# Gated linear attention in steps among the projections of the second block, tiles of two delta heads put away in DRAM, and the delta heads' norm in halves

## The chip, the cores and the metric

The kernel runs on one core of a Trainium2 chip. The metric is the device time of one execution in microseconds (us). The engines are PE (TensorE), DVE (VectorE), ACT (ScalarE), POOL (GpSimd) and SP (SyncE), which here issues all DMAs.

## What is computed

Two transformer blocks follow each other on x of 1024 tokens by 1024 features, all float32. The change touches only the mixer of the second block:

```python
proj = h @ w_in
(dn_q, dn_k, dn_v, dn_z, dn_a, dn_b, gl_q, gl_k, gl_v, gl_g, gl_r) = split(proj)
qkv = silu(causal_dwconv(concat(dn_q, dn_k, dn_v), dn_conv))
o_dn = gated_delta_rule(l2_norm(q), l2_norm(k), v, log_a, beta)          # 4 heads of 128
o_dn = rms_norm(o_dn, dn_norm_g) * silu(dn_z)
log_alpha = log_sigmoid(gl_r @ gla_w_gate2 + gla_b_gate) / 16
o_gla = gla_attention(gl_q, gl_k, gl_v, log_alpha)                       # 4 heads, keys of 64, values of 128
o_gla = rms_norm(o_gla, gla_norm_g) * silu(gl_g)
y = concat(o_dn, o_gla) @ w_o
```

In chunks of 64 tokens, gla_attention is: b = cumsum(log_alpha); att = causal((q exp(b)) (k exp(-b))^T); the state S over the chunks, S = S exp(b_last) + (k exp(b_last - b))^T v; and o = att v + (q exp(b)) S.

## The kernel before, in words

All activations lie transposed: features on the 128 partitions, 1024 tokens along the free axis. A dense product (product_steps, line 427) makes one tile of 128 output features. Weight tile and activation are each split in a high and a low part, and for each of 8 k tiles six matmuls of 512 columns run (high by high, low by high, high by low, two halves each), 48 a product. The list PLAN fixes the order of all weight tiles. At the start of product i (begin_sp, begin_act, begin_dve) SP issues the load of tile i + 5 once the low half of tile i + 2 is made, ACT casts the high part of tile i + 2 and DVE subtracts its low part. Each engine runs its own program in the written order, and semaphores tie them together. Everything in a program stands behind what is written ahead of it.

PSUM is used in four pairs of banks. Pairs 0 to 2 (the list dense) go round; a taker waits for the last reader of the pair.

The second block's mixer has these stages, one behind the other:

1. **Projections** (proj_pe, proj_act, proj_dve, proj_sp): 29 products: a small one (28: delta gates and GLA rank), then for each delta head h the tiles q (h), k (4 + h), v (8 + h), z (12 + h), then for each GLA pair hp (two heads share a tile of keys) gq (16 + hp), gk (18 + hp), two gv (20, 21 + 2 hp), two gz (24, 25 + 2 hp). Behind a q, k or v product stand a copy out of PSUM, a convolution on DVE (lines 2616, 2619), silu and, for q and k, a square on ACT (2520, 2525), a sum over partitions on PE (439), the root on ACT (453, 455) and a scaling on DVE (2625). These later parts run behind the next product (the list later). V is turned into token order (445) and scaled by beta to VT. z and gz go through silu to DRAM (spill), as gq and gk of the second pair do.
2. **Prep** (prep_*): the delta rule's triangular inverses, two rounds of four groups.
3. **Delta chunks** (delta_*): the KT tiles, then eight chunks of 128 tokens, four heads each. PE makes p1 (line 2848), DVE rd (2902), PE p2 (2855), ACT vn (2880), PE p3 and the output (2863, 2865), DVE the state S (2915), ACT the copy od (2883).
4. **GLA and norms** (gla_*, norm_*): drive interleaves three generators, one for each GLA pair and one for the four delta norms, a step of each in turn. A GLA pair has gates on PE (3022) and four passes on ACT; a scan and differences on DVE (3099 to 3109); three exponentials (3072 to 3075); kd, q and k scaled on DVE (3118 to 3121); kd turned (445); scores (3035) and their mask (3128); 15 states (3043) with two DVE updates each (3137), one PSUM pair per state; and the outputs of two heads (3052, 3055), eight groups of one matmul with att and two with the state. Then come square, sum, root, gate for each head, and the split in high and low parts for w_o.
5. **w_o** (o_*): eight products over the eight heads, in the order of O_ORDER, with the residual lanes X1 fetched from DRAM. Then the layer norm and the second FFN.

```python
            delta_pe(pe)
            drive([gla_pe(pe, 0), gla_pe(pe, 1), norms(pe, norm_pe)])
            o_pe(pe)
...
        O_ORDER = (4, 5, 6, 7, 0, 3, 1, 2)
            for c in range(15):
                r = slice(64 * (c % 2), 64 * (c % 2) + 64)
                ps = psum.take(pe, dense, f"gls{hp}{c}", ("gl_S", hp, c, 1))
```

## Time and profile before

| | us |
|---|---|
| median of 3 runs (lowest, highest) | 3825.42 (3822.31, 3826.05) |
| the profiled execution | 3833.62 |
| its span, first to last instruction | 3831.9 |
| PE busy in the span | 3604.6 (94%) |
| DVE, ACT busy | 1658.3 (43%), 1161.2 (30%) |

The profile is one execution. A matmul with float32 operands appears in it as two records, so "x16" of such a line are eight instructions; a matmul of the dense products (high and low parts) is one record. "PEclk" is the clock that TensorE was granted, as a share of its full 2.4 GHz. A value in brackets behind a row of the timeline is the idle time of that engine before it, and what it waited for.

### The profile page before, as it was taken

The page shows a single profiled execution, that of the slowest core. Times are in us where ns is not written, and L with a number is a line of the kernel's source. Part 1 is how long each engine was busy: PE and PEld are TensorE (multiplying, and loading weights), DVE is VectorE, ACT ScalarE, POOL GpSimd, SP SyncE. Part 2 cuts the span into 40 slices and gives each one's busy share as a digit, 9 for nine tenths or more (in the row PEclk, how much of TensorE's full clock was granted, in tenths as well). Part 3 has the DMA queues.
Part 4 walks back from the last instruction along what each step waited for, and adds up shares of the span by engine and source line. Part 5 has one row for each costly group of instructions (what it writes and reads, how often), then busy time and mean ns, then how long its engine had stood idle before and what let it go on. Part 6 is the DMA issues. An engine that isn't in the chain of part 4 may idle for free.

```text
span 3831.9 us, 38735 instructions
## 1 busy us (share of the span) xinstructions
PE 3604.6 (94%) x16598; PEld 2913.9 (76%) x16598; DVE 1658.3 (43%) x2021; ACT 1161.2 (30%) x1588; POOL 25.2 (1%) x69
## 2 busy tenths in 40 slices
PE   7999999989999999999999979998979899999997
PEld 5778887777766688888888757888957588888785
DVE  6544443224554333323233454317653453434354
ACT  3232213332356522111111274314332331212122
POOL 0000000000000000000000000000000000000000
PEclk9999999999999999999999999999967999999998
DMA  2214241113300121111111121120012011111111
GB/s 104 57 50 144 86 148 37 48 42 116 114 22 28 47 80 66 44 55 40 54 44 51 48 75 55 61 72 6 1 39 83 28 47 53 43 51 44 50 40 54
DMA packets 78011, 223.20 MB, mean 58 GB/s; under 512 B 12024, under 2 KB 22008, under 8 KB 77824
## 3 DMA queue, kind: packets, MB, share of 16 engines
q1 hardware_dynamic: 77840, 220.72, 17.3%
q8 instruction: 131, 2.15, 0.2%
q14 instruction: 40, 0.33, 0.0%
HBM read 196.32 MB, written 23.19 MB: 57 GB/s over the span
## 4 chain that ended last, share of the span: by engine, by line
PE 83%; DVE 8%; ACT 7%; DMA 1%; issue 1%; SPq 0%; ACTq 0%; DVEq 0%
PE PS L427 69%; PE PS L439 2%; PE PS L2725 1%; PE PS L2713 1%; PE PS L3055 1%; PE PS L1743 1%; PE PS L445 1%; PE PS L3052 1%; ACT dS L1511 1%; PE PS L1462 1%; PE PS L1765 1%; PE PS L854 1%; DVE xlo L461 1%; DVE GS L3137 1%; PE PS L2718 0%
## 5 line engine op out<-in xcount | busy, mean ns | idle before, releaser
L427 PE MATMUL PS<-xhi,whi 128*128 128x512 f32 x3120 | 997.9, 401 | 54.6 <-DVE xlo L461 43.2
L427 PE MATMUL PS<-xlo,whi 128*128 128x512 f32 x3120 | 970.1, 392 | 0.0
L427 PE MATMUL PS<-xhi,wlo 128*128 128x512 f32 x3120 | 967.9, 392 | 0.0
L427 PEld LDWEIGHTS PS<-xhi,whi 128*128 128x128 f32 x3120 | 584.9, 190 | 198.3 <-issue 55.3
L427 PEld LDWEIGHTS PS<-xlo,whi 128*128 128x128 f32 x3120 | 592.1, 190 | 126.1
L427 PEld LDWEIGHTS PS<-xhi,wlo 128*128 128x128 f32 x3120 | 590.2, 189 | 125.3
L392 DVE TENSOR_TENSOR wlo<-raw,whi 128x1024 fp32r<-128x1024 f32 (+3 forms) x307 | 329.9, 1076 | 471.2 <-ACT whi L387 471.2
L387 ACT CAST whi<-raw 128x1024 fp32r<-128x1024 f32 (+3 forms) x307 | 284.9, 929 | 514.6 <-PE PS L427 490.5
L427 PE MATMUL PS<-fhi,whi 128*128 128x512 f32 x704 | 219.3, 393 | 8.5 <-DVE flo L461 8.5
L427 PE MATMUL PS<-flo,whi 128*128 128x512 f32 x704 | 218.1, 391 | 0.0
L427 PE MATMUL PS<-fhi,wlo 128*128 128x512 f32 x704 | 218.0, 391 | 0.0
L427 PEld LDWEIGHTS PS<-fhi,whi 128*128 128x128 f32 x704 | 133.1, 190 | 37.7 <-DVE flo L461 10.2
L427 PEld LDWEIGHTS PS<-flo,whi 128*128 128x128 f32 x704 | 133.2, 189 | 28.0
L427 PEld LDWEIGHTS PS<-fhi,wlo 128*128 128x128 f32 x704 | 133.0, 189 | 27.8
L458 ACT CAST fhi<-fuv 128x1024 fp32r<-128x1024 f32 x44 | 46.2, 1050 | 328.4 <-DVE fuv L2135 221.8
L427 PE MATMUL PS<-yhi,whi 128*128 128x512 f32 x352 | 111.0, 397 | 7.6 <-DVE ylo L461 7.6
L427 PE MATMUL PS<-ylo,whi 128*128 128x512 f32 x352 | 109.8, 393 | 0.0
L427 PE MATMUL PS<-yhi,wlo 128*128 128x512 f32 x352 | 109.7, 393 | 0.0
L2202 DVE TENSOR_SCALAR fcb<-fsg,V 128x1024 f32<-128x1024 f32 x44 | 35.8, 814 | 163.6 <-ACT fsg L2178 163.6
L2218 DVE SCALAR_TENSOR_TENSOR merged<-PS,mod,merged 128x1024 f32<-128x1024 f32 x32 | 41.1, 1284 | 151.3 <-PE PS L427 151.3
L2142 DVE TENSOR_TENSOR merged<-PS,merged 128x1024 f32<-128x1024 f32 x32 | 39.2, 1225 | 137.7 <-PE PS L427 137.7
L2178 ACT COPY fsg<-PS 128x1024 f32<-128x1024 f32 x44 | 44.8, 1018 | 173.7 <-PE PS L427 173.6
(474 smaller groups left out, 3762.8 us busy)
## 6 DMA issues: line engine op xcount, KB each, us to landing
raw<-in_w_up SPq DMA_DIRECT2D x88, 512.0 KB, 3.2
raw<-in_w_in SPq DMA_DIRECT2D x67, 512.0 KB, 3.3
adr<-in_w_ada SPq DMA_DIRECT2D x48, 512.0 KB, 4.7
raw<-in_w_gate SPq DMA_DIRECT2D x32, 512.0 KB, 3.3
raw<-in_w_down SPq DMA_DIRECT2D x32, 384.0 KB, 3.1
raw<-in_w_down SPq DMA_DIRECT2D x32, 320.0 KB, 2.9
raw<-in_w_br SPq DMA_DIRECT2D x24, 256.0 KB, 2.7
spill<-wk SPq DMA_DIRECT2D x10, 512.0 KB, 4.2
```

The costliest lines, as they stand in the source:

```text
L387: act.e.copy(whis[i % RING][:, 0:kt, :], raws[i % RING][:, 0:kt, :]).then_inc(*give("w_hi", i))
L392: dve.e.tensor_tensor(wlos[i % RING][:, 0:kt, :], raws[i % RING][:, 0:kt, :], whis[i % RING][:, 0:kt, :].bitcast(F32), ALU.subtract).then_ ...
L427: ins = pe.e.matmul(ps[:, h * 512:(h + 1) * 512], w[s][:, k, :], x[:, h * 512:(h + 1) * 512], start=(at == 0 and n == 0), stop=(at == kt - ...
L439: ins = pe.e.matmul(ps[:, h * 512:(h + 1) * 512], ones, x[:, h * 512:(h + 1) * 512], start=first, stop=last)
L445: ins = pe.e.transpose(ps[:, j * 128:(j + 1) * 128], src[:, j * 128:(j + 1) * 128], ident)
L458: act.e.copy(dst, src).then_inc(*give(*signal))
L461: dve.e.tensor_tensor(dst, src, hi.bitcast(F32), ALU.subtract).then_inc(*give(*signal))
L854: ins = pe.e.matmul(o, H[m][rows, n, :], CL[m][rows, i, 1:9, :].rearrange("p a b -> p (a b)"), start=False, stop=(m == 1), skip_group_chec ...
L1462: ins = pe.e.matmul(ps[:, 64 * h:64 * h + 64], dP[u % 2][:, n, k, :], Vt[:, k0 // 128 + k, 64 * h:64 * h + 64], start=(k == 0), stop=(k == ...
L2142: dve.e.tensor_tensor(X2[:, ft, :], psum.of(j), X2[:, ft, :], ALU.add).then_inc(*give("f1_x", c, ft))
L2178: act.e.copy(GSG[v][:, FPAD:], psum.of(j)).then_inc(*give("f2_raw", v, i))
L2218: dve.e.scalar_tensor_tensor(X1[:, ft, :], psum.of(j), gt_f(ft), X1[:, ft, :], ALU.mult, ALU.add).then_inc(*give("f2_x", c, ft))
```

## The change

The order of the projections becomes a table, PROJ, in which the first GLA pair stands ahead of delta heads 0 and 1, and the second pair between heads 1 and 2 (gz tiles come behind the first z of a pair of heads). Its place in the table is called the slot. A GLA pair is cut in 13 steps, one a slot, at the head of the slot's code on each engine; the first pair starts in slot 2, the second in slot 16. The states of one step share PSUM pairs, four to a pair. Since the GLA tiles need room, q, k and VT of heads 0 and 1 are put away in DRAM in slots 8 to 15 and fetched from slot 26 on; the finished GLA heads go to DRAM too and come back as the low half XH[1] of w_o's operand, where they are split during the first four delta chunks. The norm of the delta heads is made in halves of 512 tokens: the first half of head f during chunk 4 + f, the second behind the chunks. w_o starts with the first four k tiles (the GLA heads) of three products.

The slots are: 0 small; 1 gq, 2 gk, 3 and 4 gv; 5 q0, 6 k0, 7 v0, 8 z0; 9, 10 gz; 11 q1, 12 k1, 13 v1, 14 z1; 15 to 28 the same for the second pair and heads 2 and 3.

```diff
+PROJ = [("small", 28)]
+for _hp in range(2):
+    PROJ += [("gq", 16 + _hp), ("gk", 18 + _hp), ("gv", 20 + 2 * _hp), ("gv", 21 + 2 * _hp)]
+    for _h in (2 * _hp, 2 * _hp + 1):
+        PROJ += [("q", _h), ("k", 4 + _h), ("v", 8 + _h), ("z", 12 + _h)]
+        if _h % 2 == 0:
+            PROJ += [("gz", 24 + 2 * _hp), ("gz", 25 + 2 * _hp)]
...
+        G_STEPS = ("gate", "sum", "exp", "kd", "kT", "at", "st0", "st1", "o0", "o1", "sq", "root", "d")
+        G_FROM = (2, 16)
+
+        def gla_steps(eng, gla, slot):
+            for hp in range(2):
+                if 0 <= slot - G_FROM[hp] < len(G_STEPS):
+                    gla(eng, hp, G_STEPS[slot - G_FROM[hp]])
...
+            def states(c0, n, ring):
+                ps = psum.take(pe, ring, f"gls{hp}{c0}", ("gl_S", hp, c0 + n - 1, 1))
+                pe.wait_ge("gl_kdt", hp)
+                pe.wait_ge("vt", 21 + 2 * hp)
+                for c in range(c0, c0 + n):
+                    r = slice(64 * (c % 2), 64 * (c % 2) + 64)
+                    x = 512 * (c % 2) + 256 * ((c - c0) // 2)
+                    ins = pe.e.matmul(ps[:, x:x + 256], kdt[hp][r, c // 2, :], vt[r, c // 2, :], start=True, stop=True)
+                ins.then_inc(*give("gl_s", hp, c0))
...
+        PARKED = [FT[0][0], FT[0][1], FT[1][0], FT[1][1], VT[0], VT[1]]
+        PARK_AT = {8: (0,), 9: (1,), 10: (4,), 14: (2,), 15: (3, 5)}
...
+            for slot, (kind, ft) in enumerate(PROJ):
+                gla_steps(pe, gla_pe, slot)
+                project(ft, ("sm",) if kind == "small" else (UNTIL[kind], ft))
...
+        def norm_pe(pe, ring, f, hf):
+            ps = bank.take(pe, ring, f"gn{f}{hf}", ("gn_root_ln", f, hf))
+            pe.wait_ge("gn_sq", f, hf)
+            pe.e.matmul(ps, ones, nrm[f][hf], start=True, stop=True).then_inc(*give("gn_ss", f, hf))
...
         def delta_pe(pe):
...
+                if c >= 4:
+                    norm_pe(pe, ring, c - 4, 0)
+            for f in range(4):
+                norm_pe(pe, ring, f, 1)
...
         def delta_act(act):
...
-            for s in range(10):
+            for s in range(4):
                 act.wait_ge(f"away{s}", 0)
+            begin_act(act, "w_o", 0)
             for c in range(8):
+                if c > 4:
+                    root(act, c - 5, 0)
...
+                if c < 4:
+                    other_hi(act, 4 + c)
+                else:
+                    squares(act, c - 4, 0)
+            squares(act, 0, 1)
+            squares(act, 1, 1)
+            root(act, 3, 0)
+            squares(act, 2, 1)
+            squares(act, 3, 1)
...
         def delta_dve(dve):
...
+                if c < 4:
+                    other_lo(dve, 4 + c)
+                else:
+                    gated(dve, c - 4, 0)
+                    if c > 4:
+                        normed(dve, c - 5, 0)
...
-        O_ORDER = (4, 5, 6, 7, 0, 3, 1, 2)
+        O_ORDER = (4, 5, 6, 7, 0, 1, 2, 3)
...
         def o_pe(pe):
+            first = [product_steps(pe, dense, "w_o", ft, OX, ("x1", ft), order=O_ORDER) for ft in range(3)]
+            for steps in first:
+                for _ in range(4):
+                    next(steps)
...
-            drive([gla_pe(pe, 0), gla_pe(pe, 1), norms(pe, norm_pe)])
```

The instruction order shows three places. In the changed kernel line numbers differ: 431 is 427 before, 443 is 439, 449 is 445, 391 is 387, 457 and 459 are 453 and 455.

PE, at the end of the delta chunks. Before, behind the last four output matmuls (AT by small) the GLA gates begin (g is the second gate matrix, sm the small projection):

```order
L2865 MATMUL PS<-AT_285,small_315 128x128
L2865 MATMUL PS<-AT_285,small_317 128x128
L2865 MATMUL PS<-AT_285,small_319 128x128
L2865 MATMUL PS<-AT_285,small_321 128x128
L3022 MATMUL PS<-sm_228,g_224_272 128x512 x4
```

Now, behind them, the norm sums (nrm, ones) and at once the first k tile of w_o (xhi, xlo are its operand, whi, wlo the weights):

```order
L3150 MATMUL PS<-AT_313,small_349 128x128
L3070 MATMUL PS<-nrm_364,ones_54 128x512
L3070 MATMUL PS<-nrm_359,ones_54 128x512
L3070 MATMUL PS<-nrm_361,ones_54 128x512
L3070 MATMUL PS<-nrm_363,ones_54 128x512
L3070 MATMUL PS<-nrm_365,ones_54 128x512
L431 MATMUL PS<-xhi_65,whi_60 128x512 x2
L431 MATMUL PS<-xlo_66,whi_60 128x512 x2
```

Between the delta chunks and w_o no GLA instruction is left on PE; five norm matmuls of 512 columns stand there.

PE, between two products of the projections, slots 8 to 9 (wk is the work tile of a convolution or of V, gv and kdt are values and turned keys of GLA):

```order
L431 MATMUL PS<-xhi_65,wlo_63 128x512 x2
L449 MATMUL PS<-ident_50,wk_274 128x128 x8
L2432 MATMUL PS<-gv_284,kdt_292 128x256 x7
L431 MATMUL PS<-xhi_65,whi_61 128x512 x2
```

The seven state matmuls of step st1 stand between V's transposes of slot 8 and the product of slot 9; before, only the transposes stood between products.

ACT, slot 16 (gA, gB are GLA's work tiles, gk its keys, gq its queries, whi the cast of a weight tile):

```order
L2790 ACTIVATE gq_281<-PS 128x1024
L391 CAST whi_61<-raw_58 128x1024
L2481 ACT_TABLE_LOAD
L2485 ACTIVATE gA_289<-PS,V_49 128x1024
L2487 ACTIVATE gB_291<-gA_289 128x1024
L2489 ACTIVATE gB_291<-gB_291 128x1024
L2491 ACTIVATE gB_291<-gB_291 128x1024
L2790 ACTIVATE gk_283<-PS 128x1024
```

The step's four passes stand behind the cast for product i + 2 and ahead of the copy of the slot's own product (gk).

## Rows read from the trace of the kernel before

**Rows 1.** The page, part 4: the chain that ended last, by engine.
```profile
PE 83%; DVE 8%; ACT 7%; DMA 1%; issue 1%; SPq 0%; ACTq 0%; DVEq 0%
```
**Rows 2.** Windows by stage: busy us (instructions) of each engine, granted clock, DMA.
```profile
core 0: us, PE busy (x) PEld busy (x) DVE busy (x) ACT busy (x) POOL busy (x), PEclk, DMA share, GB/s
2249.80:2585.00 335.20, 331.67 (x1458) 267.77 (x1458) 110.35 (x105) 129.28 (x129) 0.00 (x0) 0.99 0.22 75
2741.00:2784.50 43.50, 39.29 (x327) 36.99 (x326) 22.60 (x65) 16.64 (x63) 0.00 (x0) 1.00 0.01 1
2784.50:2930.20 145.70, 117.80 (x372) 82.84 (x371) 64.40 (x100) 49.07 (x52) 0.00 (x0) 0.61 0.18 69
2810.00:2823.00 13.00, 13.00 (x65) 12.78 (x64) 9.01 (x10) 4.78 (x6) 0.00 (x0) 0.50 0.00 0
...
2855.00:2913.50 58.50, 57.61 (x194) 46.01 (x194) 3.17 (x4) 3.06 (x4) 0.00 (x0) 0.50 0.05 18
...
161.20:169.40 8.20, 8.20 (x49) 6.38 (x47) 0.00 (x0) 0.00 (x0) 0.00 (x0) 1.00 0.18 71
```
**Rows 3.** Timeline at the borders of stages: start, length in us, engine, line.
```profile
2584.65 3.23 DVE L2763 TENSOR_SCALAR wb<-ones,g 128x128 f32<-128x128 f32 x16 [8.52 <-PE PS L427]
...
2585.67 3.81 PE L2685 MATMUL PS<-upper,wb 128*128 128x128 f32 x32 [1.06 <-DVE wb L2763]
...
2783.42 1.06 PE L2865 MATMUL PS<-AT,small 128*128 128x128 f32 x8
...
2930.28 1.19 PE L427 MATMUL PS<-xhi,whi 128*128 128x512 f32 x2 [5.98 <-DVE xlo L461]
```
**Rows 4.** The chain in order of time: one product of the projections; all of w_o.
```profile
2561.89 10.93 PE PS L427 x48
...
2930.28 89.97 PE PS L427 x384
```
**Rows 5.** Timeline, PE: prices of the kinds of matmul that move, and a like group.
```profile
2291.45 1.88 PE L439 MATMUL PS<-wk,ones 128*128 128x512 f32 x4
...
2262.20 1.04 PE L445 MATMUL PS<-ident,sm 128*128 128x128 f32 x8
...
2819.94 3.62 PE L3035 MATMUL PS<-gq,gk 64*128 64x128 f32 x16
...
2872.73 0.79 PE L3052 MATMUL PS<-gat,gv 128*128 128x128 f32 x2
2873.46 1.11 PE L3055 MATMUL PS<-gq,GS 64*128 64x64 f32 x4
2874.50 0.79 PE L3052 MATMUL PS<-gat,gv 128*128 128x128 f32 x2
...
162.14 0.49 PE L852 MATMUL PS<-Mk,Ug 128*128 128x128 f32 x2
162.56 0.71 PE L854 MATMUL PS<-CL,H 64*128 64x128 f32 x4
163.19 0.49 PE L852 MATMUL PS<-Mk,Ug 128*128 128x128 f32 x2
```
**Rows 6.** Timeline of the projections: the chain behind a q product of head 1.
```profile
2328.00 1.28 ACT L2528 ACT_TABLE_LOAD   x1
...
2333.46 3.92 DVE L2619 SCALAR_TENSOR_TENSOR FT<-wk,V,FT 128x1023 f32<-128x1023 f32 x3
...
2338.58 1.06 ACT L2525 ACTIVATE wk<-FT 128x1024 f32<-128x1024 f32 x1
...
2339.78 1.95 PE L439 MATMUL PS<-wk,ones 128*128 128x512 f32 x4 [0.21 <-ACT wk L2525]
...
2340.60 1.23 DVE L392 TENSOR_TENSOR wlo<-raw,whi 128x1024 fp32r<-128x1024 f32 x1 [3.22 <-ACT whi L387]
```
**Rows 7.** Timeline of the delta chunks: a chunk's last od, the next p1 and rd.
```profile
2764.37 0.27 ACT L2883 COPY wk<-PS 128x128 f32<-128x128 f32 x1 [0.18 <-PE PS L2865]
...
2764.89 1.13 PE L2848 MATMUL PS<-small,FT 128*128 128x128 f32 x8 [0.56 <-ACT wk L2883]
2765.39 1.13 DVE L2902 SCALAR_TENSOR_TENSOR small<-PS,g,VT 128x128 f32<-128x128 f32 x4 [0.89 <-PE PS L2848]
```
**Rows 8.** One line's instructions: copies of 512 columns on ACT, ns min/median/max.
```profile
L2746 ACT COPY wb<-PS x48: 586/587/588, 2608.4 to 2736.7; 128x512 f32<-128x512 f32 x48
```
**Rows 9.** Groups by line, DVE: the state updates: busy us, mean ns.
```profile
L3137 DVE SCALAR_TENSOR_TENSOR GS<-GS,gbl,PS 64x128 f32<-64x128 f32 x60 | 20.8, 347 | 22.9 <-PE PS L3043 20.1
```

More of the change, by code:

```diff
@@ L2389, in proj_sp @@
+        def proj_sp(sp):
             puts = iter(range(8))
-            def project(ft):
+            for slot, (kind, ft) in enumerate(PROJ):
                 begin_sp(sp, "w_in2", ft)
-                for _ in range(4):
-                    k = next(puts, None)
-                    if k is not None:
-                        sp.wait_ge("put", k)
-                        sp.e.dma_start(spill[:, k, :], X2[:, k, :]).then_inc(*land(f"lane{k}", "spill"))
-            def away(ft):
-                project(ft)
-                sp.wait_ge("z_out", ft)
-                sp.e.dma_start(spill[:, 8 + SLOT[ft], :], work_tile("z", ft)).then_inc(*land(f"away{SLOT[ft]}", 0))
@@ new lines, in proj_sp @@
+                if slot == 15:
+                    store_heads(sp, 0)
+                for n in PARK_AT.get(slot, ()):
+                    x = PARKED[n].rearrange("p a b -> p (a b)") if n >= 4 else PARKED[n]
+                    sp.wait_ge(*PARK_OF[n])
+                    sp.e.dma_start(spill[:, 16 + n, :], x).then_inc(*land(f"lane{n}", "park"))
+                if slot == 26:
+                    sp.wait_ge("gl_oc", 1, 1)
+                    for n in range(4):
+                        sp.wait_ge(f"lane{n}", "park")
+                        unparked(sp, n)
@@ L2629, in token @@
                 if ft < 16:
[L2630 to L2632 removed]
                     h = ft - 8
+                    if h < 2:
+                        dve.wait_ge(f"lane{h}", "spill")
+                    else:
+                        dve.wait_ge("gn_d", 4, 0)
+                        dve.wait_ge("gl_S", 0, 14, 1)
                     dve.wait_ge("beta")
@@ L2820, in build @@
         rb_ = small[16:20]
+        half = [slice(0, 512), slice(512, 1024)]
+        zD = [mem("zD", at_ft(2 * h), [128, 2, T]) for h in range(4)]
+        nrm = [[mem("nrm", heap + h * TB, [128, 512]), mem("nrm", at_ft(2 * h) + TB // 2, [128, 512])] for h in range(4)]
         def chunk(c):
@@ L2827, in group, with delta_sp @@
             return 4 * (h // 2) + c // 2, sl[2 * (c % 2) + h % 2]
+        def delta_sp(sp):
+            for r in ROUNDS[1]:
+                sp.wait_ge("pp_tx", r, 6)
+            for n in range(4):
+                sp.wait_ge(f"away{4 + n}", 0)
+                sp.e.dma_start(XH[1][:, 4 + n, :].bitcast(F32), spill[:, 12 + n, :]).then_inc(*land(f"away{4 + n}", "back"))
+            for h in range(4):
+                sp.wait_ge("rc_o", 3, h)
+                sp.e.dma_start(zD[h][:, :, 0:512], spill[:, 8 + h, :].rearrange("p (a b) -> p a b", a=2)).then_inc(*land(f"away{h}", "back"))
@@ new lines, in root, with head_hi, gated @@
+        def root(act, f, hf):
+            act.wait_ge("gn_ss", f, hf)
+            inverse_root(act, nrm[f][hf], bank.of(f"gn{f}{hf}"), 128, ("gn_root", f, hf), tables=False)
+        def head_hi(act, f, hf):
+            act.wait_ge("gn_d", f, hf)
+            if hf == 0:
+                act.wait_ge("rc_v", 7, 3)
+                act.wait_ge("rc_o", 7, 3)
+            hi_of(act, XH[0][:, f, half[hf]], od_half(f, hf), "ox_hi", f, hf)
+        def gated(dve, f, hf):
+            dve.wait_ge("od", 4 * hf + 3, f)
+            dve.wait_ge(f"away{f}", "back")
+            z = zD[f][:, hf, 0:512]
+            dve.e.scalar_tensor_tensor(z, od_half(f, hf), vec("dn_g"), z, ALU.mult, ALU.mult).then_inc(*give("gn_z", f, hf))
```

723 lines of the change are left out of this document (363 added, 360 removed).

## The prediction

> **What bounds the kernel now.** I read the chain that ended last first: PE holds 83% of the span, DVE 8%, ACT 7% [rows 1]. Time is therefore won only where PE waits or runs at its lower clock. The windows by stage show where that is [rows 2]. In the projections (2249.8 to 2585.0) PE is busy 331.7 of 335.2 us at clock 0.99: nothing to win there. The delta chunks (2741.0 to 2784.5) also run at clock 1.00. The stage behind them, 2784.5 to 2930.2, is 145.7 us with PE "busy" 117.8 us but at a mean clock of 0.61. It holds both GLA pairs and all eight norms, and it ends in a wait: the first product of w_o starts at 2930.28, the last delta matmul was running until 2784.48 [rows 3]. Inside it, 2855.0 to 2913.5 is 58.5 us of the GLA outputs alone at clock 0.50. Two things cost time here: the work itself, at half clock, and latency between PE, ACT and DVE. 117.8 us at 0.61 is about 72 us of work at full clock, so about 74 us of the stage is lost.
>
> **What the change takes away.** The stage goes. Between the last delta matmul and w_o now stand 145.8 us (2930.28 - 2784.48) [rows 3]. What stays is a tail. After the last od copy (0.3 us behind that matmul) ACT makes four half squares and one half root before PE can run the last of its norm matmuls: six half passes at 0.59 us [rows 8], 3.5 us, and some semaphore time, 4.2 us in all. The last norm matmul takes 0.94 us (two took 1.88 [rows 5]). So w_o starts about 5.7 us behind the last delta matmul. The rest of the tail (the other half roots, eight casts, the DVE halves) runs some 13 us on ACT, under the first four k tiles of three w_o products: 72 matmuls, or 1.5 products of 10.93 us [rows 4], 16.4 us. So it stays hidden. Gain 145.8 - 5.7 = **140.1 us**. w_o itself took 89.97 us for 384 matmuls, which at 10.93 us a product would be 87.4 [rows 4]: its beginning ran at half clock. After the short tail most of that goes: **2.0 us** more, at least 0 and at most 2.6.
>
> **What it adds in the projections.** PE is full there, so every matmul that moves in costs its full price, at full clock:
> - gates: four matmuls of 512 columns, 0.94 each [rows 5]: 3.8
> - transposes of kd: two sets of eight, 1.04 each [rows 5]: 2.1
> - scores: 32 matmuls of 64 rows by 128 columns. Eight (16 records) took 3.62 us at half clock [rows 5], 0.45 each, so 0.226 each: 7.2
> - states: 30 of 256 columns, half the price of 512, 0.47: 14.1
> - outputs: 32 groups of one 128-row matmul and two of 64 columns. A group took 1.77 us at half clock (2872.73 to 2874.50), so 0.885 if it scales. The nearest shape at clock 1.00 is the first block's group of L852 and two L854, 1.05 us (162.14 to 163.19), with wider matmuls [rows 5]. I take 0.95, nearer to the row of the same shape: 30.4, between 28.3 and 33.7
> - sums of squares: eight of 512 columns, 0.94: 7.5
>
> That is **65.1 us**. It agrees with the 72 us of work above, less eight such matmuls (7.5) for the delta norms.
>
> Do the waits hide? The other engines' part of the moved work is large: on DVE some 29 us a pair (30 state updates at 0.35 [rows 9], five gate passes, nine more full passes), on ACT some 21 us. They are spread over 13 slots (a slot is one product with what stands around it), and both engines were busy only 110 and 129 us of 335 [rows 2]. The tight place is the convolution chain. From the end of a product ACT copies, loads a table (2328.00), takes the root, DVE scales and convolves (2333.46, 3.92 us), ACT does silu and the square (2338.58), and PE, done with the next product, waited 0.21 us for it [rows 6]. That chain is 12.8 us and a slot of q or k is 10.93 + 1.88 = 12.8 us: no slack now. After the change the slots that carry a GLA step on PE are longer by it (1.8 to 7.6 us), which gives the chain slack just where ACT and DVE get more to do. I walked slots 5 to 14 with these durations: ACT and DVE hold GLA steps for slot n before they reach the copy of slot n, so they fit in the idle time before a product's end. I find one wait of some 0.4 us a pair, at the transposes behind slot 14 (28 for the second pair), whose own slot has no PE step: **+1 us**. One early wait of about 3 us goes, because small, gq and gk now stand in the slots where ACT also writes the residual lanes: **-3 us**, bound 0.
>
> The queues: SP now issues 12 transfers more of 512 KB (six tiles put away, six fetched), a second scan mask, and four fewer (gq and gk of the second pair, away and back). The load for product i + 5 waits, as before, for the low half of i + 2, one slot's work; of the tiles put away only V of head 1 is awaited on ACT soon after (slot 16, gate). I expect that wait to end inside slot 16, with nobody on PE needing it before slot 20. 0 us.
>
> **The border to the prep stage.** Before, the last products were gate tiles with little behind them: DVE started the first log-decay tiles at 2584.65 and PE followed at 2585.67, 1.05 us behind [rows 3]. Now the last slots are q3, k7, v11, z15. In slot 28 the silu of v11 ends about 11.3 us in; then come the cast (1.03), the low half (1.23), two passes of the GLA norm (2.5), V's tile (1.3) and four small tiles (0.8) on DVE: 18.2 us, against a product end at 10.9. PE waits 7.3 instead of 1.05 us: **+6.2 us**, bounds 2 and 10.
>
> **The delta chunks.** Between od of a chunk at 2764.37 (+0.27) and the next use of DVE at 2765.39 [rows 7] there is a gap of 0.75 us. For c below 4 ACT now casts a GLA head (1.06) and DVE subtracts (1.23) in that gap, in series: rd comes about 1.5 us late, four times: 6.0. For c = 4 to 6 PE has a norm matmul ahead of the next chunk, which waits for a half square (0.59 [rows 8]) behind the last od, then takes 0.94: 1.5 each, 4.5. The low half of w_o's third tile, now ahead of the first chunk on DVE: 0.5. **+11.0 us**, bounds 5 and 15.
>
> **Sum.** -140.1 - 2.0 + 65.1 + 1 - 3 + 6.2 + 11.0 = **-61.8 us**. The profiled execution took 3833.6 us (span 3831.9), the median of the runs is 3825.4; from the median the forecast is **3763.6 us**, from the profiled one 3771.8.
>
> **The clock, where row and rule differ.** From 2810.0 to 2823.0 PE is busy 13.0 of 13.0 us with 64-row matmuls and the granted clock stays 0.50; from 2855.0 to 2913.5 it is busy 57.6 of 58.5 us and again 0.50. Yet from 161.2 to 169.4 a like mix of L852 and L854 runs 8.2 us at 1.00 from a full start [rows 2]. So these matmuls do not bring the clock up, and whether a stretch of 7.6 us of outputs can bring it down is open. My sum takes the row at 161.2: same kind of mix, same length, full clock before it.
> The Trainium skill, page "TensorE: Matmul & The Clock Gate", Part 1, says that activity releases the throttle and that it follows how busy the PE has been. By that rule a PE that never pauses keeps its full clock, as in my sum; the trace does not agree at 2855, where a busy PE stayed at half. The other reading is the first rival.
>
> **Rivals.**
> 1. *The clock falls in the output steps.* For: the two 0.50 rows. Against: 161.2 to 169.4. Each of the four steps would take up to 14.1 us (eight groups of 1.77) instead of 7.6, and the product behind it loses the 2.6 us that w_o lost: 9.1 each, at most 36 us. If the clock falls midway, about half: 18 us. Time 3782 to 3800. Chance 0.20.
> 2. *The steps wait.* Fourteen slots carry both a GLA step and a convolution or its root; if ACT or DVE is a pass or two late in each (1.06 and 1.23 us), that is 15 to 33 us: 3779 to 3797. For: the chain had no slack. Against: ACT and DVE stood idle over 200 of 335 us. Chance 0.13.
> 3. *The other side: the convolution chain becomes the period.* If a slot's length is set by the ACT and DVE chain and not by PE, then what the two pairs add on both engines (2 x (29 + 21) = 100 us) adds to the path. It decides from 62 us on; all of it gives +38, 3864 us. The 0.21 us wait speaks for it, the low busy shares against. Chance 0.05: 0.03 for more than 7.7 us slower, 0.02 for an end close to no change.
> 4. *The tail is not hidden, so the change does not do what it says.* Eight residual lanes, four gate tiles and V tiles cross the queues near the end; if w_o's fifth k tile or the first lane waits 5 to 15 us: 3769 to 3779. Chance 0.06.
>
> The forecast's own case has 0.56: 3750 to 3775, from the bounds of its terms. The range to hold 8 in 10 reaches to most of rivals 1 and 2: **3748 to 3796**. A measurement of this kernel can tell about 0.2%, 7.7 us, from no change. Faster by more than that 0.95 (the forecast and rivals 1, 2 and 4), within it 0.02, slower 0.03 (both rival 3).
>
> **What would show each step.** The window between the last delta matmul and w_o's first: 5 to 7 us. The projections: 335 us grown to about 399, PE over 98% busy, clock 0.99; the groups of outputs at 0.9 to 1.05 us. A chunk period of 6.8 us instead of 5.26. The gap ahead of the first prep matmul: 7 us. The forecast is wrong if the windows of slots 10, 11, 24 and 25 show a clock near 0.5 to 0.8, if PE waits over 10 us in sum for ACT or DVE in the projections, or if the tail is over 10 us.

## The result, and the profile after

The changed kernel takes 3799.4 us (median of 4 runs, 3794.4 to 3802.4), the kernel before 3825.7 us beside it: ratio 0.9927, 95% interval 0.9914 to 0.9941, 26.3 us less. Run again with the experiments, it took 3795.8 against 3830.1 us (0.9907, 0.9889 to 0.9924). The forecast was 3763.6 us, a gain of 61.8: the direction was right, the gain less than half of it, and the time 3 us above the range. In the second comparison the gain is 34.3 us, a little over half, and the time at the upper end of the range; the forecast gain is 35.5 us too large by the first pair and 27.5 by the second.

The profiled execution took 3798.9 us (span 3797.1), against a span of 3831.9. The windows by stage, and six windows inside, in the trace of the changed kernel:

```profile
core 0: us, PE busy (x) PEld busy (x) DVE busy (x) ACT busy (x) POOL busy (x), PEclk, DMA share, GB/s
2249.80:2681.99 432.19, 413.99 (x1803) 328.31 (x1802) 162.60 (x198) 172.19 (x170) 0.00 (x0) 0.93 0.20 69
2375.00:2380.00 5.00, 5.00 (x32) 4.06 (x31) 1.23 (x1) 1.96 (x2) 0.00 (x0) 1.00 0.15 16
2380.00:2385.00 5.00, 5.00 (x19) 3.98 (x18) 0.00 (x0) 0.00 (x0) 0.00 (x0) 0.50 0.57 193
2385.00:2390.00 5.00, 5.00 (x13) 3.94 (x13) 0.00 (x0) 1.01 (x1) 0.00 (x0) 0.50 0.00 0
2357.50:2360.00 2.50, 1.13 (x8) 0.69 (x8) 2.21 (x7) 0.61 (x1) 0.00 (x0) 1.00 0.92 367
2360.00:2362.50 2.50, 1.31 (x7) 0.93 (x8) 2.38 (x5) 0.00 (x0) 0.00 (x0) 1.00 0.27 103
2362.50:2365.00 2.50, 2.50 (x8) 1.95 (x8) 2.37 (x6) 0.00 (x0) 0.00 (x0) 0.58 0.22 33
2681.99:2836.68 154.69, 140.12 (x1153) 137.29 (x1154) 113.72 (x235) 71.34 (x161) 0.00 (x0) 0.93 0.04 15
2836.68:2890.28 53.60, 44.10 (x336) 38.89 (x334) 33.19 (x77) 25.85 (x76) 0.00 (x0) 1.00 0.35 122
2890.28:2895.85 5.57, 4.26 (x11) 1.76 (x11) 1.77 (x3) 5.28 (x11) 0.00 (x0) 1.00 0.72 257
```

The last row answers to the 145.70 us of [rows 2]: the stage is gone. The first row shows where the gain went. The projections took 335.20 us at clock 0.99 [rows 2]; now they take 432.2 at 0.93. The clock stands at 0.50 while PE is busy all the time (2380 to 2390), and PE waits around 2360. Both are signs that the prediction had named as showing it wrong: a clock near 0.5 to 0.8 in slots 10, 11, 24 and 25 (2380 lies in slot 10), and waits of over 10 us in the projections (12.7 here, the border not counted).

The timeline of PE, first output step (2374.88 to 2384.94) and the product behind it:

```profile
2375.78 0.49 PE L2441 MATMUL PS<-gat,gv 128*128 128x128 f32 x2
2376.19 0.66 PE L2444 MATMUL PS<-gq,GS 64*128 64x64 f32 x4
2376.78 0.49 PE L2441 MATMUL PS<-gat,gv 128*128 128x128 f32 x2
...
2383.17 0.79 PE L2441 MATMUL PS<-gat,gv 128*128 128x128 f32 x2
2383.90 1.11 PE L2444 MATMUL PS<-gq,GS 64*128 64x64 f32 x4
2384.94 1.22 PE L431 MATMUL PS<-xhi,whi 128*128 128x512 f32 x2
2385.96 1.05 PE L431 MATMUL PS<-xlo,whi 128*128 128x512 f32 x2
...
2391.15 0.62 PE L431 MATMUL PS<-xhi,wlo 128*128 128x512 f32 x2
```

A group is 1.00 us at full clock (2375.78 to 2376.78); the sixth takes 1.62 and the last two 1.77, as in [rows 5]. The four steps take 10.06, 9.81, 10.11 and 9.86 us. Behind each, six or seven pairs of dense matmuls come 0.85 us apart instead of 0.45, so that the first product ends after 13.46 us instead of 10.93 [rows 4].

What PE waited for in the projections (releaser, us in sum, times, longest), and the border to the prep stage:

```profile
PE PS L2432 <- DVE GS L2540: 6.1, 4, 2.0
PE PS L2901 <- DVE wb L2982: 5.4, 1, 5.4
PE PS L431 <- ACT gk L2790: 3.0, 1, 3.0
PE PS L449 <- ACT wk L2745: 2.8, 2, 1.4
PE PS L431 <- ACT gr L457: 0.8, 2, 0.4
```
```profile
2675.49 1.07 PE L449 MATMUL PS<-ident,wk 128*128 128x128 f32 x8 [1.41 <-ACT wk L2745]
2681.99 1.41 PE L2901 MATMUL PS<-upper,wb 128*128 128x128 f32 x5 [5.44 <-DVE wb L2982]
```

Before, the first prep matmul waited 1.06 us [rows 3]. The chunks and the tail in PE's timeline, to be held against [rows 7] and [rows 3]:

```profile
2858.11 1.13 PE L3131 MATMUL PS<-small,FT 128*128 128x128 f32 x8 [0.56 <-ACT wk L3175]
...
2864.55 0.68 PE L3131 MATMUL PS<-small,FT 128*128 128x128 f32 x4 [0.56 <-ACT wk L3175]
...
2878.32 1.10 PE L3070 MATMUL PS<-nrm,ones 128*128 128x512 f32 x2 [0.98 <-ACT nrm L3075]
2879.25 1.43 PE L3131 MATMUL PS<-small,FT 128*128 128x128 f32 x8
...
2889.22 1.06 PE L3150 MATMUL PS<-AT,small 128*128 128x128 f32 x8
2891.34 2.84 PE L3070 MATMUL PS<-nrm,ones 128*128 128x512 f32 x6 [1.07 <-ACT nrm L3075]
...
2895.85 1.03 PE L431 MATMUL PS<-xhi,whi 128*128 128x512 f32 x2
```

The period of a chunk is 6.44 us up to c = 3 (2858.11 to 2864.55), 7.79 at c = 4 (2864.55 to 2872.34) and 6.91 at c = 5 and 6 (2879.25 to 2886.16); it was 5.26 before. The tail is 5.57 us.

**The balance.** Ahead of the copy of the small projection (it starts at 2251.50 before, 2248.52 after) no instruction changed; across all profiled runs with that part untouched its start lies between 2244.4 and 2252.6, so this 3.0 us is chance. From there on:

| stretch | before | after | difference | forecast |
|---|---|---|---|---|
| copy of the small projection to first prep matmul | 334.2 | 433.5 | +99.3 | +69.3 |
| prep | 154.9 | 154.7 | -0.2 | 0 |
| delta chunks | 43.9 | 53.6 | +9.7 | +11.0 |
| last delta matmul to w_o | 145.8 | 5.6 | -140.2 | -140.1 |
| w_o | 90.0 | 87.7 | -2.3 | -2.0 |
| behind w_o | 811.6 | 813.6 | +2.0 | 0 |
| sum | | | -31.8 | -61.8 |

The traces give -31.8 us and the two pairs of medians -26 and -34. The miss of 30 us lies in one row.

### The profile page after: what moved, and what is told of

It reads as the page before. It is cut to its first block and busy times, and to the rows that moved or that the text cites. A ratio compares the mean times of both kernels' runs of the same rounds, so it can differ in the third digit from the quotient of the medians.

```text
span 3797.1 us, 38785 instructions
## 1 busy us (share of the span) xinstructions
PE 3582.5 (94%) x16598; PEld 2896.2 (76%) x16598; DVE 1658.7 (44%) x2033; ACT 1169.8 (31%) x1610; POOL 25.1 (1%) x69
```

## The experiments

Theories: A, the output steps cost more than their matmuls, through the clock or through the mix of 128-row and 64-row matmuls. B, PE outran DVE's state updates. C, the delta chunks are longer by where the additions stand. D, the border is DVE's queue. The diffs below are shortened to what changes, and what stands behind a # in them is a remark. "Stretch" is the time from the small projection's copy to the first prep matmul; it is free of the chance ahead of it. The kernel before took 3826 to 3831 us in these comparisons.

| run | median us | ratio to before (95%) | stretch |
|---|---|---|---|
| e0_again | 3795.8 | 0.9907 (0.9889 to 0.9924) | 433.3 |
| e1_mixed | 3777.9 | 0.9867 (0.9851 to 0.9884) | 414.4 |
| e2_rows | 3765.7 | 0.9838 (0.9824 to 0.9853) | 402.8 |
| e3_states | 3783.5 | 0.9885 (0.987 to 0.9899) | 422.3 |
| e4_delta | 3787.5 | 0.9895 (0.988 to 0.991) | 433.6 |
| e5_sorted | 3772.4 | 0.9851 (0.9835 to 0.9867) | 410.6 |
| e6_border | 3792.9 | 0.9898 (0.988 to 0.9916) | 431.2 |
| e7_all | 3748.4 | 0.9789 (0.9773 to 0.9804) | 397.1 |
| e8_padded | 3766.4 | 0.9843 (0.9827 to 0.986) | 402.8 |
| e9_best | 3749.0 | 0.9796 (0.9782 to 0.9811) | 392.5 |
| e10_first_block | 3776.5 | 0.9869 (0.9854 to 0.9883) | 433.5 |
| e11_sorted_one_start | 3770.0 (one run) | | 404.2 |
| e12_heads | 3767.3 | 0.9837 (0.9823 to 0.985) | 396.4 |
| e13_banks | 3770.9 (one run) | | 407.3 |
| e14_all_first | 3726.6 | 0.9733 (0.9719 to 0.9746) | 392.6 |
| e15_final | 3727.7 | 0.9738 (0.9724 to 0.9751) | 386.1 |
| e16_turned | 3719.9 | 0.9723 (0.971 to 0.9736) | 386.1 |

### Does the clock fall because the outputs stand in one stretch? (e1_mixed)

```diff
 for at, k in enumerate(order or range(kt)):
+    if before is not None:
+        next(before, None)        # one group of the outputs
```

> Edit: the eight groups of each of the four output steps stand no longer in one stretch ahead of a product but one ahead of each of its eight k tiles; nothing else is moved. In the changed kernel the four steps take 10.06, 9.81, 10.11 and 9.86 us (39.8 in sum; the first five groups of the first at 1.00 us each, the last three at 1.77), and the product behind each takes about 13.45 us instead of 10.93. Theory A (a stretch of nothing but output groups brings the granted clock down, and that is most of the miss): among the dense products the clock stays at full level, the 32 groups cost 32.0 us at most and the products 10.93 each, so 7.8 + 10.1 = 18 us less than the changed kernel: about 3781 us, 0.988 of the kernel before. Rival A2 (the groups cost what they cost through their own weight loads and the low level has another cause, such as the operands or the state matmuls ahead): a slot of an output step keeps its 23.3 us, and the time stays at 3799 us. Rival A3 (interleaving only spreads the low level over the whole slot): 25 us or more a slot, 3805 us or more.

Two windows of one slot each:

```profile
2372.00:2391.00 19.00, 19.00 (x97) 15.43 (x96) 1.22 (x1) 2.98 (x3) 0.00 (x0) 1.00 0.19 55
2391.00:2410.00 19.00, 19.00 (x97) 15.38 (x97) 1.23 (x1) 2.97 (x3) 0.00 (x0) 1.00 0.09 28
```

The clock stays, a slot takes 19.1 instead of 23.5 us, and the stretch loses 19.1 us where theory A had 18. Rivals A2 and A3 fall. A group still costs 1.02 us (19.1 - 10.93, over eight): the clock is one part, not all.

### What in the mix does it? (e2_rows, e8_padded)

```diff
-ins = pe.e.matmul(ps[:, ch], GS[hp][rows, c, :], q[rows, ch], ...)
+ins = pe.e.matmul(ps[:, ch], GS[hp][:, c, :], q[:, ch], ...)
```

> Edit: the two 64-column output matmuls of each group read all 128 rows of their operands instead of the 64 rows of their head; as many matmuls, as many columns, at the same place (this mixes the two heads, so that part of the computation is changed). It asks what in the mix brings the clock down. Theory A-rows (it is the 64-row matmuls): the four steps run at 1.00 us a group to their end, 8.0 us each, and the products behind them at 10.93 us: 3781 us, 0.988 of the kernel before. Rival A-short (it is short matmuls whatever their rows): the steps stay at 9.8 to 10.1 us and the clock falls behind the fifth group as it does now: 3799 us, 0.993. Should 128 rows cost more a group at full clock, the first five groups show it: more than 1.00 us each.

```profile
2373.79 0.44 PE L2441 MATMUL PS<-gat,gv 128*128 128x128 f32 x2
2374.07 0.56 PE L2444 MATMUL PS<-gq,GS 128*128 128x64 f32 x4
2374.46 0.44 PE L2441 MATMUL PS<-gat,gv 128*128 128x128 f32 x2
```

More than either theory had: a group takes 0.67 us instead of 1.00 at the same full clock, though twice the rows are read. A step is 5.3 us, the clock stays at 1.00 in all four, and the stretch is 30.7 us shorter. So the mix of rows has a price of its own beside the clock. e8 makes the same without mixing the heads:

```diff
-dve.e.tensor_tensor(q, q, tA, ALU.mult)
+dve.e.tensor_tensor(tA[0:64], q[0:64], tA[0:64], ALU.mult)
+dve.e.tensor_tensor(q[64:128], q[64:128], tA[64:128], ALU.mult)
+dve.e.memset(q[0:64], 0.0)
+dve.e.memset(tA[64:128], 0.0)
```

> Edit: the two heads of a pair get each a scaled q of 128 rows, with zeros in the other head's 64 rows (DVE makes the product for head 0 in place of the exponent tile and for head 1 in place of q, as two passes of 64 rows and two of zeros, where one pass stood), and the output matmuls read all 128 rows of the states and of that q. The result is the reference's, unlike in the run that read 128 rows of both heads at once, which took 30.7 us less than the changed kernel from the small projection's copy to the first prep matmul (402.8 against 433.5). Theory A (the 64-row matmuls among the 128-row ones cost the switching, some 0.33 us a group, and bring the clock down): the same gain, less what the three more DVE passes a pair (some 2 to 3 us, in slots where DVE idles) bring back: 3765 to 3768 us, 0.984 to 0.985 of the kernel before; the output groups at 0.67 us and the clock at full level in all four steps. Rival (DVE's slot of that step was full): PE waits 1 to 3 us for the scores' operands in each pair, 3769 us or more.

It took 3766.4 us, with the same stretch of 402.8: theory A holds, and the extra DVE passes cost nothing.

### Switching between rows, or 64-row matmuls as such? (e5_sorted, e11_sorted_one_start)

```diff
     pe.e.matmul(... vt ..., gat ..., start=True, stop=False)     # 128 rows
+for a in range(8):
     for c in (2 * a, 2 * a + 1):                                 # 64 rows
```

> Edit: in each output step all eight 128-row matmuls come first, then all sixteen 64-row ones; the same instructions, same operands, same place, only their order. In the changed kernel a group of one 128-row and two 64-row matmuls takes 1.00 us at full clock; with 128 rows throughout it took 0.67, the clock stayed, and the kernel ran at 3765.7 us. Theory A-switch (what costs is the change between 128-row and 64-row matmuls, twice a group, some 0.16 us each, and the pauses bring the clock down): one switch pair a step is left, the step takes eight at 0.13 and sixteen at 0.14, 3.3 us, at most 5.4, the clock stays at full level and the product behind takes 10.93: 26 to 18 us less for the four steps and 10 us for the products behind, so 28 to 36 us less than the changed kernel: 3763 to 3771 us, 0.983 to 0.986 of the kernel before. Rival A-rows (64-row matmuls are slow in themselves and bring the clock down): the sixteen take 0.25 us or more each, the clock falls within the step or behind it, and the time stays above 3785 us.

The first step, its 128-row matmuls, its 64-row ones, and the product behind:

```profile
2379.03 1.95 PE L2441 MATMUL PS<-gat,gv 128*128 128x128 f32 x16
...
2383.74 1.44 PE L2445 MATMUL PS<-gq,GS 64*128 64x64 f32 x7
2385.11 1.22 PE L431 MATMUL PS<-xhi,whi 128*128 128x512 f32 x2
2386.13 1.05 PE L431 MATMUL PS<-xlo,whi 128*128 128x512 f32 x2
```

Part of both. A step takes 5.6 to 6.1 us instead of 9.8 to 10.1, so the switching is real. But the clock still fell, in the last 1.1 us of two of the four steps and right behind a third, and the gain was 23.4 us against e0, short of the 28. At full clock a step is 1.88 us for eight 128-row matmuls and 3.71 for sixteen 64-row ones: 0.235 and 0.232 each. A group of three without switching is then 0.70 us, and the other 0.30 of its 1.00 is the switching. What PE does in these 0.30 us no run shows. In e5, each start flag also made the 64-row results of other chunks in its bank overwrite instead of add, so that part of its output is not the reference's; e7 shares this. e11 has one flag a bank:

> Edit: the sorted output steps again, but only the first of the four 128-row matmuls into a bank has the start flag. In the sorted run before, each of the four had it, and the 64-row results of the chunks then did not add to what stood there, so part of its outputs was changed. The time of a step does not depend on the flag: the steps take 5.4 to 6.1 us as before, and the kernel 3772 us, within 0.2% of the sorted run. If a flagged start costs something, the 128-row part of a step becomes shorter than 1.87 us.

Its steps take 5.6 to 5.8 us, its 128-row part 1.88 us as before, and the time is 3770.0 us, as expected. The clock fell in one step of four (in two of four in e13, in one in e7), though the matmuls are the same; I found no row that says which step falls.

The Trainium skill, page "PSUM — Partial Sum Buffer", section "The four PSUM rules", says that a matmul with the start flag clears the written marks of its whole bank (of the partitions it writes), not of its own columns; e5 against e11 agrees.

### Halves of the rows, or banks? (e12_heads, e13_banks)

```diff
+for c in range(16):                 # e12: one step for both heads
+    for hh in range(2):             # upper and lower 64 rows in turn
+        rows = slice(64 * hh, 64 * hh + 64)
```
```diff
-for a in range(8):
+for a in (0, 4, 1, 5, 2, 6, 3, 7):  # e13: one head, banks in turn
```

> Edit: both heads' outputs of a pair stand in one step (the second output slot), the sixteen 128-row matmuls first, then the thirty-two 64-row ones, alternating between the heads and so between the upper and the lower 64 rows of the array; only the first matmul into a bank starts it. Sorted by head, a step took 1.88 us for its eight 128-row matmuls and 3.71 for sixteen of 64 rows and 64 columns (0.232 each, no less than the 128-row ones), while sixteen of 64 rows and 128 columns in the sorted first block, which alternate between the halves, took 2.08 (0.13 each). Theory H (matmuls on the two halves of the rows overlap): the 32 take 4.2 us, the pair 7.9 us instead of 11.2, 6.5 us less for both pairs than the sorted kernel with one start flag a bank (3770.0 us): 3763 us. It would also be why eight state matmuls, which alternate too, took 2.0 us where my step had 3.8. Rival H2 (what made them cheap there is the alternation between banks): the run beside this one, with alternating banks on one half, is as fast for each matmul. Rival H3 (neither): 7.4 us for the 32, and 3770 us or more.

> Edit: the sorted output steps with one start flag a bank, and the 64-row matmuls of a step alternate between the two banks of the result (chunk pairs 0, 4, 1, 5, 2, 6, 3, 7), two by two, on the same 64 rows of the array as before. Theory H (it is the halves of the rows that overlap): 0.232 us a matmul and 5.59 us a step at full clock as in the sorted run. Rival H2 (it is the banks): below 0.18 us for each matmul and under 4.8 us a step.

In e12, windows over the first pair's step (2384.63 to 2392.01), and the step in the timeline:

```profile
2385.00:2390.00 5.00, 5.00 (x61) 4.88 (x61) 1.23 (x1) 1.78 (x2) 0.00 (x0) 1.00 0.16 59
2390.00:2395.00 5.00, 5.00 (x51) 4.43 (x50) 0.00 (x0) 1.93 (x2) 0.00 (x0) 1.00 0.13 49
```
```profile
2384.63 3.73 PE L2441 MATMUL PS<-gat,gv 128*128 128x128 f32 x32
2388.29 3.79 PE L2446 MATMUL PS<-gq,GS 64*128 64x64 f32 x64
```

In e13, the second step, at full clock:

```profile
2391.56 1.95 PE L2441 MATMUL PS<-gat,gv 128*128 128x128 f32 x16
2393.44 3.78 PE L2445 MATMUL PS<-gq,GS 64*128 64x64 f32 x32
2397.15 0.73 PE L431 MATMUL PS<-xhi,whi 128*128 128x512 f32 x2
```

The 32 matmuls of 64 rows take 3.72 us (2388.29 to 2392.01), 0.116 each; in e13 sixteen take 3.71 (2393.44 to 2397.15), 0.232 each. It is the halves of the rows: two matmuls on different halves run side by side. Both heads cost 7.4 us instead of 11.2, the clock stayed in both pairs, and the stretch is 7.8 us shorter than e11's. The whole kernel came to 3767.3 us, within 4 us of the 3763 expected, but this is no confirmation: hardly anything of the 7.8 us reached the end. From the small projection's copy to the last instruction e12 takes 1518.5 us and e11 1518.9. The tail ahead of w_o is 11.1 us in e12 and 5.6 in e11, since PE waits 4.95 us there for ACT's root of a delta norm (L457). The same wait comes back in e15, and e16 settles its cause.

By the Trainium skill, page "TensorE: Matmul & The Clock Gate", Part 3, small matmuls whose operands lie on distinct row groups run concurrently; e12 against e13 agrees, at two for the time of one.

### The waits on the state updates (e3_states)

```diff
-    states(8, 4, [3])               # ahead of the slot's product
-    states(12, 3, dense)
+    inside = late_states()          # ahead of its 4th and 5th k tile
```

> Edit: the second state step of each pair (chunks 8 to 14) stands no longer ahead of its slot's product but inside it, the first four matmuls ahead of the fourth k tile and the other three ahead of the fifth. Theory B (PE outran the state updates of DVE: it waits 1.09 and 1.98 us in the first pair, 6.1 in sum for both, and the waits bring the clock down, so that the six matmul pairs behind them take 0.85 instead of 0.45 us each, some 2 us a pair): both waits go, DVE has 4 us more for the updates it was late with, the windows behind the transposes of the second V tile stay at full clock: 6.1 + 4 = 10 us less than the changed kernel, 3789 us, 0.9903 of the kernel before. Rival B2 (DVE's chain is the period there, with 30 updates of 0.38 us beside the convolution, and the wait only moves): the first output step then waits for the last update, and the gain is under 3 us: 3796 us or more.

```profile
2358.05 1.13 PE L2451 MATMUL PS<-gv,kdt 64*128 64x256 f32 x8
...
2360.70 1.13 PE L2451 MATMUL PS<-gv,kdt 64*128 64x256 f32 x6
```

Neither has a wait before it any more, the windows from 2355 to 2365 stand at clock 1.00, and the stretch is 11.2 us shorter (10 expected). Theory B holds; the first output step waits for nothing, so B2 falls.

### The delta chunks and the border (e4_delta, e6_border)

```diff
+if 1 <= c <= 4:
+    other_lo(dve, 3 + c)            # behind rd of the next chunk
-if c < 4:
-    other_lo(dve, 4 + c)            # behind the state updates
...
-    squares(act, c - 4, 0)          # c of 4 to 7
+    squares(act, c - 3, 0)          # c of 3 to 6
```

> Edit: the delta chunks keep every instruction but in another order. DVE takes the low half of a GLA head behind the four rd updates of the next chunk instead of behind the state updates; ACT makes the first-half square of the delta heads one chunk earlier, and DVE's gate and norm passes of c of 4 and up also stand behind rd. Before, a chunk period was 5.26 us; now it is 6.44 in the first four chunks and 6.91 in the last three. Theory C (these additions lengthen the chunks because they stand in the chain od to rd, not because an engine is full; my step said +11.0, the stretch shows +9.7): periods return to 5.3 to 5.7 us, so 4 x 1.1 + 3 x 1.4 = 8.6 us less than the changed kernel: 3791 us, 0.991 of the kernel before, the stretch from the first transposes to the last delta matmul at 45 instead of 53.6 us. Rival C2 (ACT is the chain: a vn copy waits behind cast and square whatever DVE does): periods stay above 6.2 us and the gain is under 3 us.

```profile
2847.40 1.13 PE L3131 MATMUL PS<-small,FT 128*128 128x128 f32 x8 [0.56 <-ACT wk L3175]
2852.66 1.13 PE L3131 MATMUL PS<-small,FT 128*128 128x128 f32 x8 [0.56 <-ACT wk L3175]
...
2868.16 1.02 PE L3070 MATMUL PS<-nrm,ones 128*128 128x512 f32 x2
2869.02 1.43 PE L3131 MATMUL PS<-small,FT 128*128 128x128 f32 x8
```

The period is 5.26 us again, and 5.70 with a norm matmul (2863.32 to 2869.02), which waits for nothing now. Theory C holds. The stretch is unchanged, and from the first prep matmul to the end the kernel takes 1105.6 instead of 1115.1 us.

```diff
-elif step == "d":
+elif step == "root":                # last pass of the GLA norms on DVE
```

> Edit: DVE makes the last pass of the GLA norms (two full passes of 1.22 us a pair) one slot earlier, where it now idles 8.8 us (2659.6 to 2668.4), instead of in the last slot, where they stand at 2677.46 and 2678.59 between the low half of the next weight tile and V's tile. Theory D (the border to the prep stage is DVE's queue, as my step said: 5.4 us of waiting ahead of the first prep matmul, of which these two passes are 2.4): the wait falls to 3.0 us: 2.4 us less than the changed kernel, 3797 us. Rival D2 (the wait is set by the silu of the last V tile, which the transposes wait for): it stays above 4.5 us, and the time does not change.

The wait ahead of the first prep matmul is 3.17 us instead of 5.44 and the stretch 2.1 us shorter. The medians (3792.9 against 3795.8) can't tell this by themselves; the wait can. Theory D holds.

### The first block (e10_first_block)

```diff
-pe.e.matmul(o, Ug..., Mk..., start=True, stop=False)
+pe.e.matmul(o, Ug..., Mk..., start=(j == 0), stop=False)
+for j in range(4):
+    for gl in range(2):             # then all of 64 rows, halves in turn
```

> Edit, in the first block only: in each of the four output steps of its state-space part (eight groups of one 128-row matmul and two of 64 rows by 128 columns, 1.05 us a group at full clock in the changed kernel, 161.83 to 170.18) the eight 128-row matmuls come first, then the sixteen of 64 rows; only the first matmul into a bank starts it. Theory A-switch (the change between 128-row and 64-row matmuls costs some 0.16 us each way): of 32 groups 28 pairs of switches go, 28 x 0.33 = 9 us less than the changed kernel if the clock stays: 3788 us. If the run of 64-row matmuls brings the clock down behind it, as it does in the second block's steps, 4 x 2.5 us come back and the time does not change. If there is no price of switching, nothing changes at all; the windows of these steps tell the three apart.

Windows over two of its four output steps and what lies between them; a step took 8.35 us before the edit (161.83 to 170.18):

```profile
160.18:164.14 3.96, 3.96 (x49) 3.72 (x47) 0.00 (x0) 0.00 (x0) 0.00 (x0) 1.00 0.43 169
164.14:166.66 2.52, 2.52 (x16) 1.98 (x15) 0.00 (x0) 2.00 (x3) 0.00 (x0) 1.00 0.01 3
166.66:170.62 3.96, 3.96 (x50) 3.72 (x48) 2.09 (x1) 0.00 (x0) 0.00 (x0) 1.00 0.00 0
```

A step is 3.96 us, 4.4 less, and four make 17.6: twice the 9 expected, since the 64-row matmuls alternate between the halves here and overlap once they stand together (sixteen in 2.08 us, 0.13 each). How much of the 17.6 is overlap and how much the switching, this run does not tell apart. The clock stayed. The kernel took 19.3 us less than e0, and its stretch in the second block is unchanged.

### All together (e7_all, e9_best, e14_all_first, e15_final, e16_turned)

> Edit: the sorted outputs, the second state step inside its product, the delta chunks in the other order and the earlier last norm pass, all together. If the four causes are separate, their gains add: 28 to 36 + 10 + 9 + 2.4 = 49 to 57 us less than the changed kernel, 3742 to 3750 us, 0.978 to 0.980 of the kernel before. If DVE or ACT becomes the bound in the shorter slots (a slot of an output step shrinks from 23.4 to 14.2 us), PE waits for the convolution or the gate tile's buffer, and the sum falls short by the size of those waits: over 3755 us.

e7 has sorted outputs, e3, e4 and e6: 3748.4 us, 47 less than e0, just short of the 49 to 57.

> Edit: the zero-filled q of 128 rows, the second state step inside its product, the delta chunks in the other order and the norms' last pass a slot earlier, all together. With the sorted outputs in place of the zero-filled q the same set ran at 3748.4 us, where the sorted outputs alone saved 23.4 us against the changed kernel of the same call; the 128-row ones saved 30.7 to 33.7. So 8 us less than that if the causes add: 3740 us, 3736 to 3745, 0.977 of the kernel before. If the first output step now waits for the last state update of DVE (it stands in a slot that is 7 us shorter), 3745 us or more.

e9 has the outputs of e8 instead: 3749.0 us, no better than e7, where I expected 3740. My error was the base: I added the full difference of the two output forms as e5 had it, with the clock falling at three steps; in e7 it fell at one only. So e9's stretch is 4.5 us under e7's and not 8, and in the profiled executions chance ahead of the stretch took back 3.4 of it. Against its own parts e9 adds up: its stretch is 10.3 us under e8's, and behind it 1105.7 us stand.

> Edit: the four edits of the best version so far (zero-filled q of 128 rows, second state step inside its product, delta chunks in the other order, norms' last pass a slot earlier; 3749.0 us) and the sorted steps of the first block (20 us less than the changed kernel, its steps at 3.96 instead of 8.35 us). The two lie in different stages, so the gains should add: 3729 us, 3724 to 3735, 0.974 of the kernel before. If the first block's gain had come from the clock of later stages and not from its own steps, less than 15 us are added: 3735 us or more.

e9 and e10 together: 3726.6 us, 22 under e9. The gains add.

> Edit: as the best version so far (3726.6 us), with both heads' outputs in one sorted step on alternating halves of the rows in the place of the zero-filled q. By the stretch from the small projection's copy to the first prep matmul the alternating kernel stood 6.5 us ahead of the zero-filled one (396.35 against 402.84), so the same 6.5 us here: 3720 us, 3715 to 3725, 0.972 of the kernel before. If the shorter slot lets a wait for DVE or ACT appear that the longer steps hid, 3725 us or more.

e14 with the outputs of e12: the stretch is 6.5 us shorter, and the time is the same. PE, e15, at the start of w_o:

```profile
2823.65 1.19 PE L440 MATMUL PS<-xhi,whi 128*128 128x512 f32 x2 [4.94 <-ACT nrm L469]
```

It is the wait of e12 again. My explanation was that two more takes of the dense ring had shifted which PSUM pair w_o's first product gets.

```diff
+dense.append(dense.pop(0))          # at the end of the projections
```

> Edit: the ring of the three result pairs of the dense products is turned by one place at the end of the projections; no instruction is added. In the version with both heads' outputs in one step (3727.7 us) two more places of that ring are taken, one a pair, so the first product of w_o got the two banks on which ACT's last roots of the delta norms still read: PE waits 4.9 us there for ACT, and part of the gain of the projections (386.05 against 392.56 us) was lost again. With three turns the ring stands as in the version of 3726.6 us. If that is the cause, the wait goes: 5 to 6.5 us less, 3721 us, 3717 to 3725, 0.9715 of the kernel before. If the wait comes from ACT's own order (the roots late for another reason), it stays at 4 to 5 us and so does the time, 3727 us.

The wait is gone (the tail is 4.6 us instead of 10.1), so that was the cause, and the kernel takes 3719.9 us, the fastest of all: 106.5 us under the kernel before.

## Why the prediction missed

By its steps, in the order of the sum:

- **The stage that goes, w_o:** right: -140.2 and -2.3 us against -140.1 and -2.0. The tail stayed hidden (5.57 us, forecast 5.7).
- **The delta chunks:** right in mechanism and size: +9.7 us of +11.0, and e4 shows that it is the order, as the step said.
- **The border:** 5.4 us of wait where the step had 7.3, by the two GLA norm passes and V's tile on DVE; for the two passes e6 shows it (2.3 us).
- **The moved work, outputs:** this term failed. 30.4 us were forecast; the four steps took 39.8, and the products behind them lost some 10.7 more. The group's price was near (1.00 us at full clock against 0.95), but 0.30 of it is switching between 128 and 64 rows, which e5 and e11 measure and the prediction did not see. The forecast of 0.95 lay near the measured 1.00 because its row, the first block's group, has the same switching in it. And the sentence "My sum takes the row at 161.2: same kind of mix, same length, full clock before it" chose the wrong row: the clock fell behind the fifth group of each step. That was the first rival, at its "falls midway" size of 18 us (chance 0.20); e1 took 19.1 back by keeping the clock. The Trainium skill, page "TensorE: Matmul & The Clock Gate", Part 1, says that activity releases the throttle and that the clock follows how busy the PE has been. If busy is what the profile calls busy, the trace does not agree: 5.00 of 5.00 us at 1.00, then 5.00 of 5.00 at 0.50.
- **The moved work, states:** busy 9.5 us instead of 14.1. Successive chunks lie on different halves of the rows, which overlap (e12). This error ran the other way and hid 4.6 us of the miss. The other kinds are within 1.0 us (scores 8.2 for 7.2, sums of squares 7.2 for 7.5).
- **The waits:** "I find one wait of some 0.4 us a pair" was wrong. I had laid out the engines' parts by slot and missed that the two matmul groups of the second state step wait for the updates of the first: DVE makes 16 in 6.11 us, behind a convolution. 6.1 us of waits, and some 3.9 us of low clock behind them; e3 took 11.2 us back. The transposes wait 2.8 us where the step had +1, the products behind the GLA roots 0.8.
- **The early wait** of 3 us did not go (3.0 us, until ACT's copy of gk): ACT works without a pause there, 4.6 us on the residual lanes and then, ahead of that copy, 5.6 us on the first pair's gate step (2269.62 to 2275.21). The reordering that was to free these slots put the gate step into one of them; no run moved either part alone. The step's bound was 0.

Together, for outputs, the products behind them, states, scores, sums, waits on states, the low clock behind these, transposes, roots, early wait and border: 9.4 + 10.7 - 4.6 + 1.0 - 0.3 + 6.1 + 3.9 + 1.8 + 0.8 + 3.0 - 1.9 = 29.9 us, the 30.0 of the balance. The second rival (waits, 15 to 33 us) and the first each came in partly. I gave them chances of 0.20 and 0.13 as alternatives, when both could come in the same run; their sum belonged into the range.

## What to carry to other kernels

A mix of 128-row and 64-row matmuls had a price of its own here, 0.30 us a group: try to sort them by rows, to fill up to 128 rows with zeros, or to put 64-row matmuls on alternating halves. In the first block sorting gave 17.6 us in its four steps (19.3 in the medians) without a change to any operand. When a stage's work is moved into the slots of a full engine, walk the consumer's backlog at the moment each producer starts, not the mean load of a slot. And where rings of buffers are shared, count the takes: two more of them put a 4.9 us wait ahead of w_o and hid a gain of 7.8 us in e12 and of 6.5 us in e15.

## What the runs showed of the hardware that was not expected

- A group of one 128-row and two 64-row matmuls took 1.00 us in turn and 0.70 sorted, at full clock; with 128 rows throughout 0.67. In the first block (64 rows by 128 columns) it took 1.04 in turn and 0.495 sorted.
- Matmuls of 64 rows took 0.232 us each on one half of the rows and 0.116 on alternating halves.
- The granted clock fell in all four mixed output steps though PE did not pause, in or right behind seven of the sixteen sorted ones in e5, e7, e11 and e13, and in no output step with 128 rows throughout (e2, e8), on alternating halves (e12), or spread among the dense products (e1). In the first block's mixed steps (8.4 us at 1.04 a group) it stayed at 1.00.
